# Two experts' rows summed on chip, the first expert's rows by products, and output parts between state-space steps, in a two-block model on one core

## The chip, the cores and the metric

The kernel runs on one core of a Trainium2 chip. A core has a matrix engine (TensorE, PE in the rows, with PEld for its weight loads), three engines for elementwise work (VectorE, DVE; ScalarE, ACT; GpSimd, POOL), one that issues transfers (SyncE, SP), 16 DMA engines, an on-chip memory of 128 partitions and matmul banks of 128 x 512 float32. The metric is the time of one execution of the whole program on the device, in microseconds (us); less is better. All data are float32.

## The reference

Two transformer blocks for 512 tokens of 1024 channels. The first is an RWKV-7 mixer beside banded attention. The second is a mixer of three parts (a state-space mixer with 8 heads in 4 chunks, forgetting attention, a gated convolution) whose 1024 channels go through an output matrix, and then a mixture of 32 experts. What the change touches:

```python
    y = jnp.concatenate([y_ssd, y_att, y_cnv], axis=-1)      # 512 + 256 + 256 channels
    x = x + g_m * (y @ w_out)
    h = rms_norm_2(x, norm_ffn_g) * (1.0 + sc_f) + sh_f
    # router: a group by softmax of h @ w_rg, two of its 8 experts, two weights for each token
    for each expert e (32):                                   # on the rows of h that chose it
        hid = silu(xb @ w_gate[e]) * (xb @ w_up[e])           # 1024 -> 512
        ys  = hid @ w_down[e]                                 # 512 -> 1024
    x = x + g_f * (sum over a token's two experts of weight * ys)
    out = rms_norm_2(x, final_norm_g)
```

## The kernel before, in words

**Order.** Each engine runs its own hand-written list (`pe_block2`, `dve_block2`, `pe_experts` and so on) and waits on semaphores where it needs another's work. Matmul banks are handed out by a plan that is made before the program: `plan(name, by)` gives the next fill a bank and says which engine empties it, `plan_held(name)` keeps a bank for a later fill, `fill`, `begin`, `take` and `empty` carry it out.

**Second block, its end.** `ssd_rows(i)` (L2062, L2064) is the state-space step of a pair of heads, i = 0 to 3; it needs the operands that VectorE makes (`s_gm`). Behind each step VectorE gates the rows with z (`ssd_gated`, L2225 to L2228), ScalarE squares them (L1906), and after two steps TensorE sums the squares (`both(("snorm", g), ...)`, L2036, L2037), from which `yT` tiles 0 to 3 are made (L2323). Tiles 4 to 7 of `yT` (attention and convolution) are ready earlier (`s_m1free`). The output matrix is loaded by SyncE (L573, four loads of 1 MB, semaphore `s_wo`) once `s_m1free` is up. `pe_out` makes the output for four token tiles of 128 rows in halves of 512 columns: `pe_out_part(i, t, half, bank, ks, first, last)` (L763) is the product over the channel tiles `ks`. For the first tile `first_tile` makes channels 4 to 7 of both halves, then the sums of squares, then channels 0, 1 and 2, 3. For each tile VectorE adds the gated result to X (L1679, L1680), ScalarE makes the row norm, VectorE scales the rows into `xn_tiles` (L743), GpSimd stores them to memory (`xn_dram`), and TensorE transposes them (L757) for the router's logits (L2095).

**Router.** VectorE makes from the logits, for each of 8 sets of 128 choices (two choices, four tiles), the expert tile `hot_tile` and the position in it `hot_pos` as one-hot rows (L2472 to L2474). A matrix product of the two (L2125) gives `slots`, the token of each of 64 positions of each expert; a second (L2131) gives `places`, where each result row goes. Experts with more than 64 rows get extra tiles (`extras`, `overflow`): 16 at most.

**Experts.** Three weight slots of 12288 columns hold gate/up (`wgu`, two loads of 2 MB each, L2592) and down weights (`wdn`, one load of 2 MB, L2596) of experts e, e+1, e+2. The first two slots are loaded once the router's inputs in them are dead (`s_slots` 2), the third when the block's end is through (`s_slots` 3); later ones when gate/up or down of the expert three before is done. For an expert GpSimd gathers 64 rows of `xn_dram` (L2657), TensorE turns them (`turn_rows`, L2734), VectorE scales them (`rows_in`, L2897, L2899), TensorE makes gate and up (L2744), ScalarE and VectorE the hidden rows, TensorE turns them (L2751) and makes down (L2760), VectorE gates the result (L2921), and GpSimd scatters it to `y_dram` (L2665). TensorE works on expert e's gate/up before e-1's down.

**The end.** The last expert's result is not scattered: a selection matrix (`last_hot`, turned by L2843) times the weights puts its rows where they belong (`add_last`, L2819). The other results are loaded back (L2638); VectorE adds tiles 0 to 2 to X (L2982), TensorE adds X (`add_x`, L2812) and does tile 3 with diagonals (L2837). ScalarE and VectorE norm the rows (L2960, L2974), which go out (L2642).

## Time and profile before

| | us |
|---|---|
| median of three runs | 1473.2 (1470.58 to 1477.06) |
| the profiled execution | 1470.04 |
| its span, first to last instruction | 1468.0 |
| last output part and router logits, to | 905.7 |
| first gate/up product starts | 936.66 |
| last gate/up product ends | 1438.5 |

The profile is one execution. A row of the timeline has start, duration, engine, line of the kernel, operation, what it writes and reads, its shape and how many instructions are merged; in brackets stands how long the engine was idle before it and what ended that. A float32 matmul is two records.

### The profile page before, as it was taken

To read this page: it belongs to the slowest core of one execution; us is meant where nothing else is said; L and a number is where in the kernel's file an instruction comes from. 1 tells how busy PE (TensorE), PEld (TensorE's weight loads), DVE (VectorE), ACT (ScalarE), POOL (GpSimd) and SP (SyncE) were. 2 spreads that over 40 slices of the span, in tenths; PEclk is the share of its full clock that TensorE was granted. 3 is DMA by queue.
4 is the path that set the end of the run, shared out by engine and by line. 5 is a ranking of instruction groups with operands and counts; after the bars stand their busy time and mean duration, and the time that the engine had idled before them with its cause. 6 is when DMAs were issued, how large, how long until landed. Compare 5 with 4: busy or idle time off the path is not lost.

```text
span 1468.0 us, 21300 instructions
## 1 busy us (share of the span) xinstructions
PE 1328.4 (90%) x7646; PEld 658.7 (45%) x7647; DVE 572.7 (39%) x1078; ACT 345.2 (24%) x745; POOL 158.7 (11%) x273
## 2 busy tenths in 40 slices
PE   5989999999999989998999896699899878998887
PEld 2445656568844444446455444333333322333222
DVE  1366373735123343468566734322212121122124
ACT  2222232321234432211454421011101010111012
POOL 4011111102020000000000001211111111111110
PEclk9999999999999999998999997699989999999999
DMA  9151607051171100121110384169999999999994
GB/s 353 72 202 42 256 2 287 2 201 32 30 243 56 33 15 0 34 86 44 58 58 1 129 372 193 36 273 393 401 420 417 408 402 419 423 393 409 411 389 198
DMA packets 40768, 300.71 MB, mean 205 GB/s; under 512 B 8840, under 2 KB 8992, under 8 KB 23792
## 3 DMA queue, kind: packets, MB, share of 16 engines
q1 hardware_dynamic: 32704, 285.12, 49.4%
q0 software_dynamic: 7984, 14.50, 3.3%
q8 instruction: 53, 0.87, 0.2%
q14 instruction: 27, 0.22, 0.0%
HBM read 296.08 MB, written 13.73 MB: 211 GB/s over the span
## 4 chain that ended last, share of the span: by engine, by line
PE 72%; DMA 17%; DVE 7%; issue 2%; ACT 1%; POOL 0%; SPq 0%; DVEq 0%; ACTq 0%; POOLq 0%
PE bank L832 21%; DMA arena<-in_w_down 12%; PE bank L2744 10%; PE bank L763 8%; PE bank L2760 7%; PE bank L878 4%; DVE arena L2167 3%; DMA arena<-in_w_gu 3%; PE bank L841 2%; PE bank L821 2%; DMA arena<-in_w_ada 2%; PE bank L2734 1%; DMA arena<-in_ada_w 1%; PE bank L1060 1%; PE bank L1076 1%
## 5 line engine op out<-in xcount | busy, mean ns | idle before, releaser
L832 PE MATMUL bank<-hT,arena 128*128 128x512 f32 x768 | 341.7, 600 | 0.0
L2744 PE MATMUL bank<-arena,hT 128*64 128x512 f32 x1024 | 233.9, 606 | 24.2 <-DMA arena<-in_w_gu 22.7
L832 PEld LDWEIGHTS bank<-hT,arena 128*128 128x128 f32 x768 | 144.6, 192 | 177.3 <-issue 174.9
L2744 PEld LDWEIGHTS bank<-arena,hT 128*64 128x64 f32 x1024 | 72.0, 139 | 164.4 <-issue 139.1
L2760 PE MATMUL bank<-arena,yT 128*64 128x512 f32 x512 | 128.7, 649 | 14.5 <-DMA arena<-in_w_down 14.4
L763 PE MATMUL bank<-arena,yT 128*128 128x512 f32 x256 | 114.4, 602 | 2.3 <-DVE yT L1633 2.3
L2904 DVE TENSOR_SCALAR hT<-hT 128x256 f32<-128x256 f32 x32 | 9.4, 294 | 247.1 <-ACT hT L2855 247.1
L763 PEld LDWEIGHTS bank<-arena,yT 128*128 128x128 f32 x256 | 48.2, 193 | 60.5 <-issue 56.2
L2760 PEld LDWEIGHTS bank<-arena,yT 128*64 128x64 f32 x512 | 36.7, 148 | 82.3 <-issue 64.6
L878 PEld LDWEIGHTS bank<-arena 64*64 64x64 f32 x1856 | 59.3, 135 | 27.9 <-issue 14.4
L2855 ACT ACTIVATE hT<-bank 128x256 f32<-128x256 f32 x32 | 12.3, 383 | 246.2 <-PE bank L2744 246.2
L878 PE MATMUL bank<-arena 64*64 64x64 f32 x1856 | 63.9, 220 | 6.5 <-POOLq L673 3.9
L821 PE MATMUL bank<-arena,cactB 128*32 128x512 f32 x288 | 46.0, 665 | 19.5 <-DMA arena<-in_w_ada 17.6
L672 POOL TENSOR_TENSOR arena<-arena 128x512 f32<-128x512 f32 x20 | 29.3, 1467 | 280.6 <-DVEq L1540 194.1
L2921 DVE TENSOR_TENSOR hT<-bank,masks 128x512 f32<-128x512 f32 x32 | 22.1, 692 | 76.7 <-PE bank L2760 76.7
L1808 ACT ACTIVATE arena<-bank 128x512 f32<-128x512 f32 (+4 forms) x53 | 26.0, 491 | 93.4 <-PE bank L832 78.3
L2863 ACT ACTIVATE yT<-bank 128x256 f32<-128x256 f32 x32 | 12.3, 383 | 146.3 <-PE bank L2751 146.3
L2167 DVE SCALAR_TENSOR_TENSOR arena<-arena,cols 128x512 f32<-128x512 f32 x60 | 45.1, 752 | 2.1
L2734 PEld LDWEIGHTS bank<-ident,yT 64*128 64x128 f32 x256 | 30.7, 201 | 33.6 <-issue 33.6
L841 PE MATMUL bank<-arena,hT 128*128 128x128 f32 x384 | 44.0, 276 | 0.0
L841 PEld LDWEIGHTS bank<-arena,hT 128*128 128x128 f32 x384 | 43.4, 192 | 1.3 <-issue 1.1
L2662 POOL CAST place_col<-iotas 128x1 uint32 (+1 forms) x34 | 6.2, 183 | 344.0 <-DVE hT L2921 258.1
(471 smaller groups left out, 1592.1 us busy)
## 6 DMA issues: line engine op xcount, KB each, us to landing
arena<-in_w_gu SPq DMA_DIRECT2D x64, 2048.0 KB, 30.7
arena<-in_w_down SPq DMA_DIRECT2D x32, 2048.0 KB, 36.6
arena<-in_w_in SPq DMA_DIRECT2D x55, 512.0 KB, 3.7
arena<-in_ada_w SPq DMA_DIRECT2D x24, 1024.0 KB, 5.0
arena<-in_w_ada SPq DMA_DIRECT2D x8, 1024.0 KB, 9.1
arena<-in_w_out SPq DMA_DIRECT2D x8, 1024.0 KB, 14.3
arena<-in_w_ada SPq DMA_DIRECT2D x8, 512.0 KB, 4.7
arena<-expert_rows SPq DMA_DIRECT2D x4, 1024.0 KB, 8.4
```

The lines of the kernel that those rows point to most:

```text
L672: done(G.tensor_tensor(Lfc[l % 2], LTc, level_up[:, l:l + 1, 0:HD].to_broadcast([P, 8, HD]), MUL))
L763: ins = T.matmul(bank[:, :], yT[:, k, CH(t)], w_outs[i][:, k, 512 * half:512 * half + 512], start=first and not m, stop=last and m == len( ...
L821: last = T.matmul(banks[ADA_BANK][32 * j:32 * j + 32, :], cactB[:, c0 + k, :], ada_slots[slot][:, j * 512:(j + 1) * 512], start=k == 0, st ...
L832: last = T.matmul(bank[0:rows, :], w[:, k, 0:rows], hT[:, k, :], start=k == 0, stop=k == KD - 1)
L841: last = T.matmul(bank[:, CH(t)], src[:, k, CH(t)], w[:, k, :], start=k == 0, stop=k == KD - 1)
L878: last = T.matmul(bank[r, BK(m)], stat[r, m, :], mov[r, m, :], start=True, stop=True)
L1808: empty(S, "act", S.activation(dst, bank[:, :] if src is None else src(bank), kw.pop("func", ACT.Copy), **kw), name)
L2167: dve.done(V.scalar_tensor_tensor(cv[:, i, :], un[:, i, j:j + SEQ], w(j), cv[:, i, :], MUL, ADD))
L2734: last = T.transpose(banks[bank][:, MT * k:MT * k + MT], tile.xg[:, k::KD], ident[0:MT, 0:MT])
L2744: last = T.matmul(banks[1 + ub][MT * h:MT * h + MT, :], tile.xT[:, k, :], wgu[u][:, k // 4, :, k % 4, 256 * h:256 * h + 256], start=k == 0 ...
L2760: last = T.matmul(banks[5 + (u if db is None else db)][MT * q:MT * q + MT, :], tile.hidT[:, j, h, :], wdn[u][:, a, 512 * q:512 * q + 512], ...
L2921: V.tensor_tensor(tile.yo, banks[5 + u][:, :], gate_rows, MUL).then_inc(steps.rows, 1)
```

## The change

Three things are changed, and what makes room for them.

1. Output parts. In the second block the product over channels 4 to 7 of the first token tile no longer runs after the four state-space steps: half 0 runs before step 2, half 1 before step 3, with the wait for the output matrix in front of half 0. Where they stood, channels 4 to 7 of the second tile's half 0 run. Two banks are held for the two halves from those points and one for the third part.
2. First rows. The first expert's 64 rows are not gathered: a selection matrix `first_hot` (two VectorE steps, `hot_of`) times the four normalised token tiles, which now stay on chip in four buffers, gives them turned (32 products of 64 columns). GpSimd gathers from expert 1 on. The second places matrix goes: the slot matrix now holds the choice as well (tokens numbered to 1024), so its values give the places of one half of the columns, and a repeat of it on the other 64 rows, behind the products, gives the other half. Results are laid out choice by choice in `y_dram`.
3. Two last experts. Expert 30's result is not scattered either; both have their selection matrices turned (now just before the last gate/up product, with the final gain's spreading) and are added by `add_last`. The gate/up weights of expert 31 are requested before the down weights of 30.

For room: `gate2` and `out_tmp` move into slot 1's part of the arena, so slot 1's down weights and slot 2's gate/up weights wait for the block's end and slot 2's down weights for the first rows.

```diff
@@ plan
+            if i >= 2:
+                plan_held(("out", 1, 0, i - 2))
             plan(("ys", i), "dve")
...
+        plan_held(("out", 1, 1, 0))
@@ pe_out
+                    begun = (i, t, half) == (1, 1, 0)
+                    pe_out_part(i, t, half, fill(("out", i, t, half)), range(4 if begun else KD), not begun, True)
@@ pe_block2
+                if i == 2:
+                    eng.wait_ge(s_wo, 128)
+                    eng.wait_ge(s_m1free, 1)
+                if i >= 2:
+                    pe_out_part(1, 0, i - 2, begin(("out", 1, 0, i - 2)), (4, 5, 6, 7), True, False)
                 ssd_rows(i)
@@ first_tile
                 two = [fill(("out", 1, 0, half), 1 + half) for half in range(2)]
-                eng.wait_ge(s_m1free, 1)
-                for half in range(2):
-                    pe_out_part(1, 0, half, two[half], (4, 5, 6, 7), True, False)
+                pe_out_part(1, 1, 0, begin(("out", 1, 1, 0)), (4, 5, 6, 7), True, False)
                 eng.wait_ge(s_ysq, 4)
@@ dve_router
             eng.sem_inc(s_hot, 1)
+            hot_of(0, first_hot)
+            eng.sem_inc(s_hot, 1)
...
+        def hot_of(e, out):
+            dve.done(V.scalar_tensor_tensor(hot_last, hot_pos, 0.0, hot_tile[:, :, e:e + 1].to_broadcast([P, KT, MT]), ALU.is_gt, MUL))
+            dve.done(V.tensor_tensor(out, hot_last[:, 0:TT, :], hot_last[:, TT:KT, :], ADD))
@@ sp_experts
-            for u in range(U):
-                eng.wait_ge(s_slots, 2 if u < 2 else 3)
-                load_gate_up(u, u)
-                load_down(u, u)
+            eng.wait_ge(s_slots, 2)
+            load_gate_up(0, 0)
+            load_down(0, 0)
+            load_gate_up(1, 1)
+            eng.wait_ge(s_slots, 3)
+            load_down(1, 1)
+            load_gate_up(2, 2)
+            eng.wait_ge(tiles[0].xf, 2)
+            load_down(2, 2)
@@ pe_experts
+            eng.wait_ge(s_hot, 2)
+            for k in range(KD):
+                for t in range(TT):
+                    last = T.matmul(banks[ROWS_BANK][:, MT * k:MT * k + MT], xn_tiles[1][t][:, k::KD], first_hot[:, t, :],
+                                    start=t == 0, stop=t == TT - 1)
+            last.then_inc(tiles[0].xf, 1)
+            for by in ("act", "dve"):
+                eng.wait_ge(emptied[by], len(given[by]))
+            for n in range(KT):
+                last = T.matmul(banks[4][MT:P, 0:NE + NOV], hot_pos[:, n, :], hot_tile[:, n, :], start=n == 0, stop=n == KT - 1)
@@ after the last expert
             add_x(3, False)
+            eng.wait_ge(first.rows, NE - 1)
+            add_last(0, 0, start=True)
+            add_last(0, 3)
+            eng.wait_ge(first.hidT, NE)
+            add_last(0, 1, start=True)
             finish(LAST[0], LAST[1], NE - 1)
```

The order of TensorE's instructions around the third state-space step (L2051 are the decay rows ahead of it, L2062 and L2064 the step itself), before against after:

```order
 L2064 MATMUL bank<-arena 64x128
 L2051 MATMUL bank<-cactB,side 128x512 x2
+L762 MATMUL bank<-arena,yT 128x512 x4
 L2062 MATMUL bank<-arena 64x128 x3
 L2064 MATMUL bank<-arena 64x128
```

The output part L762 (before L763) now stands between decay rows and step. On TensorE from the slot matrix to the first gate/up product, before (slot matrix, places matrix, the last expert's selection, the turning of the gathered rows, gate/up):

```order
L2125 MATMUL bank<-hT 64x48 x8
L2131 MATMUL bank<-hT 64x48 x16
L2843 MATMUL bank<-ident,hT 64x128 x8
L2734 MATMUL bank<-ident,yT 128x64 x8
L2744 MATMUL bank<-arena,hT 64x512 x16
```

and after (slot matrix, products, second half of the places, gate/up, turning of the extra tile's rows):

```order
L2127 MATMUL bank<-hT 64x48 x8
L2734 MATMUL bank<-hT,arena 128x64 x32
L2740 MATMUL bank<-hT 64x48 x8
L2759 MATMUL bank<-arena,hT 64x512 x16
L2749 MATMUL bank<-ident,side 128x64 x8
```

32 products have come in, eight transposes, eight products and the selection have gone. At TensorE's end, before (turning of the hidden rows, X, down, X, selections, X, diagonals):

```order
L2751 MATMUL bank<-ident,hT 128x128 x2
L2812 MATMUL bank<-X,ident 128x512 x2
L2760 MATMUL bank<-arena,yT 64x512 x8
L2812 MATMUL bank<-X,ident 128x512 x2
L2819 MATMUL bank<-hT,yT 128x512 x4
L2819 MATMUL bank<-hT 128x512 x4
L2812 MATMUL bank<-X,ident 128x512 x4
L2837 MATMUL bank<-arena 128x512 x4
```

and after:

```order
L2766 MATMUL bank<-ident,hT 128x128 x2
L2833 MATMUL bank<-X,ident 128x512 x2
L2841 MATMUL bank<-hT,arena 128x512 x6
L2775 MATMUL bank<-arena,yT 64x512 x8
L2841 MATMUL bank<-hT,arena 128x512 x2
L2833 MATMUL bank<-X,ident 128x512 x2
L2841 MATMUL bank<-hT,arena 128x512 x2
L2833 MATMUL bank<-X,ident 128x512 x2
L2841 MATMUL bank<-hT,arena 128x512 x4
L2833 MATMUL bank<-X,ident 128x512 x2
L2841 MATMUL bank<-hT,arena 128x512 x2
L2860 MATMUL bank<-arena 128x512 x4
```

Three selections of two products have come in front of the last down product (L2775), and five stand behind it instead of four.

## Rows read from the trace of the kernel before

**Rows 1.** The page's first line.

```profile
span 1468.0 us, 21300 instructions
```

**Rows 2.** Busy by stretch: us, engines' busy us (records), TensorE clock, DMA share, GB/s.

```profile
902.00:905.70 3.70, 3.60 (x16) 3.49 (x16) 0.00 (x0) 0.00 (x0) 3.32 (x3) 0.50 0.79 266
...
936.00:942.00 6.00, 5.34 (x14) 1.65 (x16) 0.60 (x1) 0.00 (x0) 3.91 (x8) 0.50 0.20 72
942.00:948.00 6.00, 6.00 (x34) 2.55 (x31) 0.12 (x1) 0.38 (x1) 0.39 (x2) 0.94 0.08 22
...
976.00:1424.00 448.00, 398.44 (x1818) 143.81 (x1817) 99.62 (x191) 50.78 (x127) 72.15 (x123) 0.95 1.01 408
1424.00:1438.00 14.00, 12.25 (x52) 3.83 (x52) 1.17 (x3) 1.09 (x2) 2.27 (x4) 1.00 0.50 207
```

**Rows 3.** Timeline, state-space steps 2 and 3 to the new tile's transposes.

```profile
822.51 1.15 PE L2062 MATMUL bank<-arena 128*64 128x128 f32 x8 [4.29 <-issue]
...
831.03 0.68 PE L2062 MATMUL bank<-arena 128*64 128x128 f32 x8 [2.87 <-issue]
...
832.74 7.13 PE L763 MATMUL bank<-arena,yT 128*128 128x512 f32 x16
...
841.42 13.90 PE L763 MATMUL bank<-arena,yT 128*128 128x512 f32 x32
855.16 1.05 PE L757 MATMUL bank<-ident,arena 128*128 128x128 f32 x8
...
835.99 0.75 DVE L2227 SCALAR_TENSOR_TENSOR arena<-arena,cols,bank 128x512 f32<-128x512 f32 x1
...
837.55 1.38 ACT L1906 ACTIVATE arena<-arena 128x512 f32<-128x512 f32 x2 [0.90 <-DVEq L2229]
...
851.87 0.75 DVE L743 TENSOR_SCALAR arena<-X,small 128x1024 f32<-128x1024 f32 x1 [1.88 <-ACTq L721]
```

**Rows 4.** The four loads of the second output matrix: min/median/max, first and last start.

```profile
L573 SPq DMA_DIRECT2D arena<-in_w_out x4: 379/470/741, 810.5 to 811.9; - x4
...
DMA to landing us min/median/max: 5.0/11.1/14.1
```

**Rows 5.** Timeline, router to the first gate/up product, and two shapes elsewhere.

```profile
921.25 1.94 PE L2125 MATMUL bank<-hT 128*64 128x48 f32 x16 [6.97 <-DVEq L2476]
924.89 3.26 PE L2131 MATMUL bank<-hT 128*64 128x48 f32 x32 [1.70 <-DVEq L2488]
...
923.23 0.20 DVE L2481 TENSOR_SCALAR side<-bank 64x48 f32<-64x48 f32 x1 [1.72 <-PE bank L2125]
...
929.27 0.69 DVE L2495 SCALAR_TENSOR_TENSOR hT<-hT,side 128x512 f32<-128x512 f32 x1
...
936.66 10.08 PE L2744 MATMUL bank<-arena,hT 128*64 128x512 f32 x32 [1.51 <-DVE hT L2899]
...
902.09 3.60 PE L2095 MATMUL bank<-side,hT 128*128 128x36 f32 x16 [1.69 <-ACT hT L727]
...
146.62 2.00 PE L996 MATMUL bank<-arena 128*128 128x64 f32 x16
```

**Rows 6.** SyncE's issues, the last load's landing, and the timeline's end.

```profile
L2592 SPq DMA_DIRECT2D arena<-in_w_gu x3: 333/353/425, 958.2 to 975.6; - x3
...
1407.66 0.33 SPq L2596 DMA_DIRECT2D arena<-in_w_down  x1
...
DMA to landing us min/median/max: 32.2/32.2/32.2
...
1434.89 3.65 PE L2744 MATMUL bank<-arena,hT 128*64 128x512 f32 x16 [1.39 <-DMA arena<-in_w_gu]
...
1444.91 3.65 PE L2760 MATMUL bank<-arena,yT 128*64 128x512 f32 x16
1448.50 1.98 PE L2812 MATMUL bank<-X,ident 128*128 128x512 f32 x4
...
1452.23 1.88 PE L2819 MATMUL bank<-hT 64*128 64x512 f32 x8
...
1457.58 3.60 PE L2837 MATMUL bank<-arena 128*128 128x512 f32 x8
```

More of the change, by code:

```diff
@@ L775, in pe_out @@
                 for half in range(2):
-                    pe_out_part(i, t, half, fill(("out", i, t, half)), range(KD), True, True)
+                    begun = (i, t, half) == (1, 1, 0)
+                    pe_out_part(i, t, half, fill(("out", i, t, half)), range(4 if begun else KD), not begun, True)
                     if t and not half:
@@ L2125, in pe_block2 @@
                 last = T.matmul(bank[0:MT, 0:NE + NOV], hot_pos[:, n, :], hot_tile[:, n, :], start=n == 0, stop=n == 2 * TT - 1)
-            full(last)
-            eng.wait_ge(s_hot, 2)
-            bank = fill(("places",))
-            for q in range(2):
-                for n in range(2 * TT):
-                    last = T.matmul(bank[MT * q:MT * q + MT, 0:NE + NOV], hot_pos[:, n, :], hot_tile[:, n, :], start=n == 0, stop=n == 2 * TT - 1)
             full(last)
@@ L2493, in dve_router, with place_rows, dve_places @@
+        def place_rows(rows, bank):
+            b = bank[rows, 0:NE + NOV]
+            dve.done(V.tensor_scalar(r_place[rows], b, 0.0, 8192.0, ALU.is_equal, MUL))
+            return V.scalar_tensor_tensor(r_place[rows], b, 2.0, r_place[rows], MUL, ADD)
+        def dve_places(eng):
+            eng.wait_ge(s_spread, 1)
+            dve.done(place_rows(slice(MT, P), banks[4]))
+            dve.done(V.tensor_scalar(places, r_place, half_row, None, ADD))
             eng.sem_inc(s_routed, 1)
-            done(V.tensor_tensor(r_q, hot_tile[:, :, NE - 1], wts.rearrange("p k t -> p (k t)"), MUL))
@@ L2581, in extras @@
                     body(o)
+        ROWS_BANK = 7 if bank_of[fill_at[("slots",)]] == 0 else 0
         def sp_experts(eng):
@@ L2797, in body, with spread @@
                     turn_rows(tiles[u1], first, e + 1, it1)
-                if not begun and not last:
+                if last:
+                    eng.wait_ge(s_copied, 1)
+                    overflow(it, u, e)
+                if not begun:
                     finish(it0, u0, e - 1)
-                if last:
-                    eng.wait_ge(s_copied, 2)
-                overflow(it, u, e)
-            def spread_gain():
+                if not last:
+                    overflow(it, u, e)
+            def spread():
                 eng.wait_ge(s_gateB, 16 + 48)
                 for half in range(2):
-                    spread = T.matmul(banks[4 * half][:, :], ones_row, gain_row[:, 512 * half:512 * half + 512], start=True, stop=True)
-                spread.then_inc(s_spread, 1)
+                    T.matmul(banks[half][:, :], ones_row, gain_row[:, 512 * half:512 * half + 512], start=True, stop=True)
+                eng.wait_ge(s_routed, 3)
+                for j in range(2):
+                    for t in range(TT):
+                        for q in range(2):
+                            ins = T.matmul(banks[3 + 2 * j][MT * q:MT * q + MT, CH(t)], last_hot[j][:, t, :], ident[:, :], start=True, stop=True)
+                ins.then_inc(s_spread, 1)
             def add_x(t, stop):
@@ L2839, in sums @@
                 ins.then_inc(s_x3, 1)
-            eng.wait_ge(s_routed, 3)
-            for t in range(TT):
-                for q in range(2):
-                    turned = T.matmul(banks[6][MT * q:MT * q + MT, CH(t)], last_hot[:, t, :], ident[:, :], start=True, stop=True)
-            turned.then_inc(s_spread, 1)
-            turn_rows(tiles[0], first, 0, 0)
             experts(eng, body)
```

172 lines of the change are left out of this document (76 added, 96 removed).

## The prediction

> **What bounds the kernel now.** I read the page's first lines, then the busy shares by stretch, then the SyncE issues, and only then the instructions at the joints. The span is 1468.0 us [rows 1]. Over the stretch from 976 to 1424 us the DMA engines' share is 1.01 at 408 GB/s with TensorE busy 398 us of 448 [rows 2]: the 32 experts' weights stream, 6.3 MB each, sets the pace there. A stream shortens only if it starts earlier or carries less. It starts when slot 0 comes free: the gate/up loads of expert 3 go out at 958.2 and those of expert 4 at 975.6, when slots 0 and 1 are read [rows 6]. So three joints count: the path of TensorE and VectorE before the router (a later router is a later stream), the path from the slot matrix to the end of the first gate/up product, and what follows the last weights, which were issued at 1407.66 and landed 32.2 us later, at 1439.9, here called T [rows 6]. Anything else that the change moves is under the stream.
>
> **The change, part by part: the moved output parts (term A).** Two groups of eight matmul records move in front of the state-space steps 2 and 3, where TensorE idled 4.29 and 2.87 us [rows 3]; a third group of eight moves from tile 1 into the wait for the second norm. Work of 512 columns takes 0.43 us a record at the full clock (13.90 us for 32) [rows 3], so a group is 3.4 us. But the first group now stands behind the wait for all of `w_out`, and step 2 stands behind the group. The last of those four loads was issued at 811.9 and took 14.1 us: it lands at 826.0 [rows 4], 3.5 us after step 2 began. TensorE, which finished its decay rows at 818.2, would idle 7.8 us and come back at the low clock, as it did after the 4.29 us (eight records of step 2 in 1.15 us, against 0.68 us for step 3's) [rows 3]. Between 3.4 us (all at 2.4 GHz) and 6.9 us (all at 1.2 GHz, twice the time) I take 6.0 us for the group, since the first gate/up product, begun at 936.66, ran about 6 us low before it sped up (granted clock 0.50 to 942, 0.94 behind it) [rows 2, 5]. Then: 826.0 + 6.0 = 832.0; step 2, 1.8 us as step 3 took (831.03 to 832.8), 833.8; first norm's sums 1.7, 835.5; second group 3.4, 838.9; step 3 1.8, 840.7; third group 3.4, 844.1. VectorE and ScalarE need 2.9 us after step 3 for gating and squares (835.99 to 838.93 in the trace) [rows 3], so 843.6: hidden. Second norm's sums 1.7 give 845.8, the sixteen records left of tile 0 6.9 give 852.7, and the last eight of tile 1's first half 856.1. The transposes behind them wait for tile 0's normalised rows, which came 4.3 us after its last product (848.3 to 852.6) [rows 3], so 857.0 plus a semaphore; before they began at 855.16. Term A is +2.0 us, ends -0.4 (group all at the full clock: TensorE alone decides) and +2.9. From there to the router the order is the same and TensorE has no idle time, so it carries over in full. The gate row's load moves past the output weights' wait, the normalised rows have four buffers instead of two: both cost nothing, since the rows' VectorE step waited 1.9 us for ScalarE and not for a store [rows 3].
>
> **The first rows by products (term B).** Before, from the end of the slot matrix (921.25 + 1.94 = 923.2) came: half-row fix-up, places matrix (32 records, 3.26 us), the turned selection, the gather, eight transposes, two VectorE steps, and the first gate/up product at 936.66 [rows 5]: 13.5 us. Now: 32 products of 64 columns against 128x128 weights, 64 records. At the full clock such a shape ran 16 records in 2.00 us, hence 8.0 us; at the low clock the nearest shape, 36 columns against the same weights, ran 16 in 3.60 us, hence 14.4 us [rows 5]. I take 14.4: the granted clock was 0.50, the level of 1.2 GHz, in every stretch read from 902 to 942, also in the 3.7 us in which those records kept TensorE 97% busy (3.60 of 3.70) [rows 2]. Behind the products the second places matrix (16 records at 0.10) and VectorE's two steps run side by side, 1.7 us. The first gate/up product then starts at 923.2 + 14.4 + 1.7 = 939.3, not 936.66, and takes the same 10.08 us, as it again begins low. Term B is +2.6 us. Its ends: rising after 6 us of work, 27 records at 0.225 and 37 at 0.125 are 10.7 us, start 935.6, product 7.0 us, together -4.1; full clock throughout, 8.0 us, -6.9. The high end is a strided read of the weights 10% slower, +4.0. The two added VectorE steps for the first selection (0.69 us, as the step at 929.27 does for the last, and one of half the size) lie in VectorE's 1.72 us wait for the slot matrix [rows 5]; without that cover they'd cost 1.2. The extra expert's gather goes out some 6 us earlier, since GpSimd no longer waits for the places matrix; the two scatters of zero rows and the two last selections (about 3 us of VectorE) end before the first gate/up product does. After it, the next joints (overflow product, down, second gate/up) are unchanged, so A + B shifts the stream.
>
> The Trainium skill, in "TensorE: Matmul & The Clock Gate", section "Part 1: The HAM clock gate", says that what warms the array is a time of sustained matmul work, whatever the number of matmuls. By it 14 us of back-to-back products would not stay low and term B would be -4.1; the low row of 36 columns speaks against it but is short. This is the second case below.
>
> **Weight order at the start.** Slot 1's down and slot 2's gate/up wait for the block's end now: 6.3 MB, 15.4 us at 408 GB/s, from about 904 to 920, and slot 2's down goes out after the products, 5.1 us. All three are there long before their experts. Nothing.
>
> **Two last experts on chip (term C).** Expert 30's scatter and its return through memory go, 0.26 MB or 0.6 us of stream. The gate/up weights of expert 31 now come before the down weights of 30: they land at T-10, and one 2 MB load is 5.1 us. TensorE: gate/up 31 (3.65 us a half) is done by T-5; down 30 runs from T-5.1 to T-1.4; transposes 0.7; X of tile 3 1.9; three selections of expert 30 at 0.94 (1.88 us for two) [rows 6] end at T+4.0; down 31, which could start at T, ends at T+7.6. Before it ended at 1448.5, T+8.6. Then gating 0.8, five selections 4.7, three X products 5.5 and the last diagonal 3.6 give T+22.2 against 1461.2, T+21.3: +0.9, less 0.6 of stream: +0.3 us. Ends: -3.7, if the 4.0 us in front of down 31 find room before T; +5.6, if one more spread (1.8 us) and four more selections (3.8 us) all stand in the path. The result loads no longer stand behind expert 30's scatter but behind that of 29, and find half-idle DMA engines (share 0.50 from 1424 to 1438) [rows 2]; but TensorE's chain from down 31 on has no idle time in it [rows 6], so this gives nothing by itself.
>
> **Sum.** +2.0 + 2.6 + 0.3 = +4.9 us on the profiled execution of 1470.04 us (span 1468.0): 1474.9. The median of the three runs is 3.2 us above that execution, so against it I predict 1473.2 + 4.9 = 1478.1 us. A measurement of this kernel can tell about 0.5%, 7.4 us, from no change; the forecast is inside.
>
> **The rivals.** (1) The clock rises during the products: term B is -4.1 and the time 1473.2 + 2.0 - 4.1 + 0.3 = 1471.4. For it: 14 us of unbroken work; against: the stretch at 902. (2) Slower: the tail. TensorE alone decides the end after T, and the change gives it more to do there. It decides from the point at which its queue is still busy when the last weights land; I have it 4.0 us late already. If nothing of the added work hides, term C is +5.6 and the time 1483.4. For it: the last 12.7 us before were one unbroken row of TensorE work [rows 6]; against: TensorE waited 1.39 us and more at each load just before. (3) The moved parts do fill the gaps, because `w_out` lands earlier than in the trace: up to 6.9 us leave the path and the time is 1473.2 - 6.9 + 2.6 + 0.3 = 1469.2. Against it stand the landing row and the wait in front of the group. (4) The tail's added work all finds room before T: term C is -3.7 and the time 1474.1. Faster by over 0.5% takes (1) and (3) together, 1462.5; (1) and (4) give 1467.4.
>
> **How the numbers follow.** Forecast 0.50, (1) 0.22, (2) 0.14, (3) 0.06, (4) 0.08. The range takes in (1), (3) and the high end of terms A and B (1478.1 + 0.9 + 1.4) and (2): 1468 to 1484 us. Above 1480.6 lie most of (2) and about a fifth of the forecast, together 0.23; under 1465.8 two good surprises at once, 0.07; the rest, 0.70, is within 0.5%.
>
> **What would show it.** Term A: TensorE idle until the output weights land, near 826, step 2 ending near 834 and the first transposes of the new tile near 857. Term B: the products' 64 records take 14 us at granted clock 0.50 and the first gate/up product starts about 4.6 us later than 936.66; about 10 us and a clock of 1 are rival 1. The stream: expert 4's gate/up load goes out near 980 and the last weights land near 1444. Term C: the last diagonal product ends some 22 us after that. I am wrong if the DMA share between these falls below 1, since the shift would then not carry over, or if the last weights land earlier than 1440.

## The result, and the profile after

The changed kernel takes 1475.22 us (median of 20 runs, 1472.58 to 1483.85), the kernel before beside it 1469.76 us (20 runs, 1467.45 to 1477.22). The ratio is 1.0043, with a 95% interval of 1.0028 to 1.0058: slower by 4 to 8.5 us. Its middle lies inside the 0.5% that the prediction calls no change, its upper end a little outside. The forecast was +4.9 us, 1478.1 us in a range of 1468 to 1484. The total held; whether the terms did is the question of all that follows.

The first line and three stretches of the profile after (us, busy us of TensorE, its weight loads, VectorE, ScalarE, GpSimd, then TensorE clock, DMA share, GB/s), which answer to [rows 1, 2]:

```profile
span 1476.9 us, 21405 instructions
...
976.00:1424.00 448.00, 396.13 (x1820) 143.00 (x1818) 96.82 (x186) 49.58 (x124) 74.38 (x125) 0.96 0.99 404
982.30:1430.30 448.00, 395.77 (x1818) 142.89 (x1817) 99.03 (x191) 50.39 (x126) 72.21 (x122) 0.96 1.01 409
1424.00:1438.00 14.00, 13.64 (x78) 6.73 (x76) 3.69 (x8) 3.66 (x8) 1.17 (x2) 0.88 0.77 327
```

The prediction gave a DMA share below 1 as a sign of being wrong, and from 976 to 1424 us it is 0.99. But that stretch begins 6.3 us earlier in this stream than it did in the kernel before, whose fifth expert's load went out at 975.58, against 981.87 here. Moved by those 6.3 us (second row), the share is 1.01 at 409 GB/s, as before. The stream is as full, so a shift at its start can carry to its end. The profiled span is 8.9 us longer, but 5.65 us of that stand ahead of all changed code: state-space step 1 starts at 820.15 where it started at 814.50. The comparison below is therefore made from the start of step 1 (its first row in the timeline), and the other 5.65 us are taken up with the first experiment.

The timeline of TensorE after, from the first moved part to the logits (answers to [rows 3]):

```profile
820.15 0.71 PE L2062 MATMUL bank<-arena 128*64 128x128 f32 x8
...
831.15 5.99 PE L762 MATMUL bank<-arena,yT 128*128 128x512 f32 x8 [7.29 <-DMA arena<-in_w_out]
837.07 0.71 PE L2062 MATMUL bank<-arena 128*64 128x128 f32 x8
...
862.44 1.16 PE L756 MATMUL bank<-ident,arena 128*128 128x128 f32 x8 [0.84 <-DVEq L743]
...
908.68 3.60 PE L2100 MATMUL bank<-side,hT 128*128 128x36 f32 x16 [1.69 <-ACT hT L729]
```

TensorE idles 7.29 us until the output weights land, and the first group takes 5.99 us. Step 2 starts 16.92 us behind step 1 (8.01 before), the first transposes of the new tile 42.29 us behind it (40.66 before), the last logits 88.53 (87.59 before).

From the slot matrix to the extra tile's gate/up (answers to [rows 5]):

```profile
927.83 1.94 PE L2127 MATMUL bank<-hT 128*64 128x48 f32 x16 [6.97 <-DVEq L2473]
929.71 15.54 PE L2734 MATMUL bank<-hT,arena 128*128 128x64 f32 x64
945.18 1.84 PE L2740 MATMUL bank<-hT 128*64 128x48 f32 x15
946.76 1.11 PE L2759 MATMUL bank<-arena,hT 128*64 128x512 f32 x1
...
946.92 7.80 PE L2759 MATMUL bank<-arena,hT 128*64 128x512 f32 x31
...
957.34 7.09 PE L2759 MATMUL bank<-arena,side 128*64 128x512 f32 x32 [0.70 <-DVE side L2918]
```

The 64 records of the products take 15.54 us, so the first gate/up product (two rows, from 946.76) starts 18.9 us behind the slot matrix instead of 15.4. But it takes 8.0 us instead of 10.08, and the extra tile's takes 7.09 instead of 8.78.

And the end (answers to [rows 6]):

```profile
1430.47 1.98 PE L2823 MATMUL bank<-yT 1*128 1x512 f32 x4
1432.38 1.30 PE L2828 MATMUL bank<-ident,yT 128*64 128x128 f32 x16
1433.46 1.93 PE L2828 MATMUL bank<-ident,hT 128*64 128x128 f32 x16
1435.17 7.73 PE L2759 MATMUL bank<-arena,hT 128*64 128x512 f32 x32
1442.72 3.60 PE L2775 MATMUL bank<-arena,yT 128*64 128x512 f32 x16
...
1448.35 2.85 PE L2841 MATMUL bank<-hT,arena 64*128 64x512 f32 x12
1451.12 3.65 PE L2775 MATMUL bank<-arena,yT 128*64 128x512 f32 x16
...
1466.40 3.70 PE L2860 MATMUL bank<-arena 128*128 128x512 f32 x8
```

In this trace neither of the two last down products waits for its weights, which landed at 1441.71 and 1446.63. That is not so in all of them. Here the turning of the selections and the gate/up product behind it met a stretch at the low clock, and in seven of the ten traces with the new end they did not. after_again (the first experiment) is one of the seven:

```profile
1440.77 3.65 PE L2775 MATMUL bank<-arena,yT 128*64 128x512 f32 x16 [0.53 <-DMA arena<-in_w_down]
...
1449.22 3.65 PE L2775 MATMUL bank<-arena,yT 128*64 128x512 f32 x16
1453.67 1.13 PE L2841 MATMUL bank<-hT,arena 64*128 64x512 f32 x4 [0.79 <-DVE hT L2940]
...
1464.50 3.70 PE L2860 MATMUL bank<-arena 128*128 128x512 f32 x8
```

There TensorE still waits 0.53 us for the down weights of expert 30, so nothing ahead of that product costs time.

### The profile page after: what moved, and what is told of

It is laid out like the page before. It is cut to its first block, busy times and chain, and to the rows that moved or that the text cites. A ratio compares the mean times of both kernels' runs of the same rounds, so it can differ in the third digit from the quotient of the medians.

```text
span 1476.9 us, 21405 instructions
## 1 busy us (share of the span) xinstructions
PE 1342.5 (91%) x7718; PEld 675.5 (46%) x7719; DVE 575.4 (39%) x1085; ACT 345.5 (23%) x745; POOL 157.7 (11%) x270
## 4 chain that ended last, share of the span: by engine, by line
PE 69%; DMA 20%; DVE 7%; ACT 2%; issue 2%; POOL 0%; SPq 0%; DVEq 0%; ACTq 0%; POOLq 0%
PE bank L832 20%; DMA arena<-in_w_down 16%; PE bank L2759 8%; PE bank L762 7%; PE bank L2775 6%; PE bank L878 4%; DVE arena L2162 3%; PE bank L841 2%; PE bank L821 2%; DMA arena<-in_w_ada 2%; PE bank L2749 1%; PE bank L2734 1%; DMA arena<-in_ada_w 1%; DMA arena<-in_w_out 1%; PE bank L1060 1%
## 5 line engine op out<-in xcount | busy, mean ns | idle before, releaser
L2775 PE MATMUL bank<-arena,yT 128*64 128x512 f32 x512 | 126.5, 639 | 14.5 <-DMA arena<-in_w_down 14.3
L762 PE MATMUL bank<-arena,yT 128*128 128x512 f32 x256 | 117.3, 612 | 9.6 <-DMA arena<-in_w_out 7.3
L762 PEld LDWEIGHTS bank<-arena,yT 128*128 128x128 f32 x256 | 49.0, 196 | 69.6 <-issue 57.2
L2775 PEld LDWEIGHTS bank<-arena,yT 128*64 128x64 f32 x512 | 36.2, 146 | 81.1 <-issue 63.6
L878 PEld LDWEIGHTS bank<-arena 64*64 64x64 f32 x1856 | 60.1, 136 | 27.8 <-issue 14.4
L1520 DVE TENSOR_TENSOR arena<-bank,arena 128x512 f32<-128x512 f32 x32 | 22.1, 692 | 52.9 <-PE bank L878 52.9
```

The costliest lines, as they stand in the source:

```text
L762: ins = T.matmul(bank[:, :], yT[:, k, CH(t)], w_outs[i][:, k, 512 * half:512 * half + 512], start=first and not m, stop=last and m == len( ...
L878: last = T.matmul(bank[r, BK(m)], stat[r, m, :], mov[r, m, :], start=True, stop=True)
L1520: empty(V, "dve", V.tensor_tensor(dst, b3(bank[:, :], HD), dst, ADD), (n, p, l))
L2775: last = T.matmul(banks[5 + (u if db is None else db)][MT * q:MT * q + MT, :], tile.hidT[:, j, h, :], wdn[u][:, a, 512 * q:512 * q + 512], ...
```

## How the runs are compared

All joints below are taken from each run's own TensorE and SyncE timelines. "A" is from the start of step 1 to the start of the last logits, "B" from the start of the slot matrix to the issue of the fifth expert's first gate/up load, "C" from that issue to the end of the span. From the logits to the slot matrix it is 19.15 to 19.17 us in every run but the three with fillers (20.2 to 20.5).

| kernel | A | B | C | ratio to before, 95% interval |
|---|---|---|---|---|
| before | 87.59 | 54.33 | 492.4 | |
| after | 88.53 | 54.04 | 495.0 | 1.0043 (1.0028 to 1.0058) |
| after_again | 88.53 | 54.01 | 495.8 | 1.0012 (0.9990 to 1.0035) |
| a_off | 89.00 | 53.99 | 492.8 | 1.0025 (1.0004 to 1.0046) |
| a_late | 86.04 | 53.73 | 494.7 | 1.0000 (0.9981 to 1.0020) |
| c_off | 88.73 | 54.11 | 500.0 | 1.0059 (1.0038 to 1.0080) |
| b_gather | 88.52 | 46.52 | 495.3 | 0.9968 (0.9945 to 0.9991) |
| warm | 88.53 | 55.63 | 494.0 | 1.0075 (1.0046 to 1.0104) |
| gather_late | 85.02 | 46.95 | 495.3 | 0.9965 (0.9947 to 0.9983) |
| all_warm | 86.02 | 55.45 | 496.2 | 1.0027 (1.0005 to 1.0048) |
| c_undo | 88.50 | 53.99 | 491.3 | 1.0004 (0.9978 to 1.0031) |
| best | 85.11 | 46.67 | 491.7 | 0.9950 (0.9921 to 0.9978) |
| straight | 88.59 | 53.21 | 494.4 | 1.0009 (0.9981 to 1.0037) |
| straight_warm | 88.81 | 45.38 | 493.6 | 0.9991 (0.9966 to 1.0016) |

In the first pair the sum is +0.94 (A), -0.29 (B) and +2.6 (C), +3.25 us. The times alone can't carry much: an interval of 0.2% to either side is 3 us, and the recorded ratio and the quotient of the two medians differ by up to 0.2% (after_again: 1.0012, and 1474.97 over 1470.06 is 1.0033). What is concluded below rests on joints, and the times are used as a bound.

## Experiment 1: the changed kernel again (after_again)

> The changed kernel once more, beside the kernel before on the same chip, for a second trace. In the first pair of traces the changed kernel was already 5.65 us late at the first state-space step of block 2, ahead of anything that was changed there. Theory R (block 1 just varies from run to run): the time is 4 to 6 us above before, but this offset is another one, inside -3 to +3 us. Theory L (something of the change reaches back into block 1, by the place of data or code): it is again 4 us or more. From that step on both say the same: +0.9 us at the router's logits, +0.6 at the fifth expert's load, +3.3 at the end.

Measured: 1474.97 us, ratio 1.0012; step 1 starts at 817.54, 3.0 us later than in the trace of before, and not 5.65. From there A, B and the sum to the end (657.5 against 656.75) repeat to 0.7 us. Over the thirteen traces that share the changed kernel's block 1, step 1 starts between 813.2 and 825.6 (a_late and best), and a_late, with the same block 1 as the others, is 1.3 us earlier than before. So the offset comes and goes from one execution to the next, as theory R has it. This run alone would not have told, since 3.04 us lies between R's 3 and L's 4. Whether some 2 to 3 us of it are lasting stays open, since the median of the thirteen is 817.1 against one trace of before; the gap between the two medians (5.5 us) is 2.2 us more than the 3.25 us that the changed code shows.

## Experiments 2 and 3: the moved output parts

The first puts the parts back behind the four steps:

```diff
-                if i == 2:
-                    eng.wait_ge(s_wo, 128)
-                    eng.wait_ge(s_m1free, 1)
-                if i >= 2:
-                    pe_out_part(1, 0, i - 2, ...)
...
-                pe_out_part(1, 1, 0, ...)
+                eng.wait_ge(s_m1free, 1)
+                for half in range(2):
+                    pe_out_part(1, 0, half, two[half], (4, 5, 6, 7), True, False)
```

> The changed kernel with the output parts back behind the four state-space steps (part 1 of the change undone). Forecast theory, term A: the parts ahead of steps 2 and 3 cost because the first one waits for the output weights; the logits then come earlier by 0.9 us (what the first pair of traces shows) to 2.0 us (what the sum had), and the time falls by as much. Rival: the cost beside the wait is that the second tile's first half is begun early and finished late; then undoing brings no more than 0.3 us.

Measured: the logits come 0.47 us later, not earlier, and the time is the same (1.0025 against 1.0012, intervals that overlap). Yet its TensorE order is that of the kernel before, whose logits came 1.4 us sooner. The difference arises in step 3 alone. Timeline and stretch of a_off, and the stretch of before (us, TensorE busy, granted clock, DMA share, GB/s):

```profile
833.67 1.15 PE L2058 MATMUL bank<-arena 128*64 128x128 f32 x8 [2.61 <-issue]
...
833.60:836.80 3.20, 3.13 (x29) 0.52 0.00 0
```

```profile
831.00:832.70 1.70, 1.67 (x28) 1.00 0.00 0
```

The same 28 records ran at 1.2 GHz here and at 2.4 GHz there; from step 1 to the start of step 3 both took 16.5 us. So by the trace of before part 1 costs 0.9 us, by a_off's it gains 0.5. Its price is about nothing, and the clock's level in step 3 decides its sign. The expected 0.9 to 2.0 us did not come.

The second keeps the wait for the output weights out of step 2's way:

```diff
-                if i == 2:
+                if i == 3:
                     eng.wait_ge(s_wo, 128)
                     eng.wait_ge(s_m1free, 1)
-                if i >= 2:
-                    pe_out_part(1, 0, i - 2, ...)
+                    pe_out_part(1, 0, 0, ...)
...
+                pe_out_part(1, 0, 1, two[1], (4, 5, 6, 7), True, False)
                 pe_out_part(1, 1, 0, ...)
```

> The changed kernel, but no output part ahead of state-space step 2; half 0 stands ahead of step 3, where the output weights have landed, half 1 and the third part stand in the wait for the second norm. Forecast theory (term A is the wait for the weights): step 2 starts 8.0 us behind step 1, not 16.9, the logits come 2.5 us earlier (1 to 4), and the time falls by that, since one group of 3.4 to 6 us now fills TensorE's 2.87 us of idleness ahead of step 3. Rival (the groups' own time is the cost, the wait is not): logits and time move by less than 0.5 us.

```profile
821.20 1.15 PE L2062 MATMUL bank<-arena 128*64 128x128 f32 x8 [4.28 <-issue]
...
826.95 3.60 PE L762 MATMUL bank<-arena,yT 128*128 128x512 f32 x8
830.47 0.71 PE L2062 MATMUL bank<-arena 128*64 128x128 f32 x8
```

Measured: step 2 is back at 8.0 us behind step 1, and the group ahead of step 3 runs in 3.60 us with no idle time before it; step 3 starts 17.3 us behind step 1, against 24.0 in the changed kernel. The logits come 2.5 us sooner here and in all_warm, 3.4 and 3.5 in best and gather_late, which have the same edit: 85.0 to 86.0 us in the four, 88.5 to 88.8 in the eight with part 1 as changed. The time is 1471.1 against 1475.0 us, ratios 1.0000 and 1.0012, with intervals that overlap. The expectation held in the trace: the wait for the weights is what ate the gain of the other parts. (The edit also moves half 1 into the wait for the second norm, which no run does by itself.)

## Experiment 4: the first rows gathered again (b_gather)

```diff
-            for k in range(KD):
-                for t in range(TT):
-                    last = T.matmul(banks[ROWS_BANK][:, MT * k:MT * k + MT], xn_tiles[1][t][:, k::KD], first_hot[:, t, :], ...)
...
-            gather(tiles[1], 1, 1, s_picked[0], 0)
+            for u in range(2):
+                eng.wait_ge(tiles[u].xf, 1)
+                gather(tiles[u], u, u, s_picked[0], u)
...
+            turn_rows(tiles[0], first, 0, 0, ROWS_BANK)
```

> The changed kernel with the first expert's rows gathered from memory and turned again, the gather issued right behind the slot matrix; no products with the selection. Forecast theory (term B is the products at the low clock): slot matrix to gather's issue 4.3 us, landing 3.2 us later, turning and scaling 2.5 to 3.0 us, so the first gate/up product starts 10.5 us behind the slot matrix's start instead of 18.9, takes 10 us instead of 7.9, and ends 6.3 us earlier; the time falls by 6 us. Rival (the stream is not set by this joint): the first gate/up ends early, but the fifth expert's load goes out at the same time as before and the time moves by less than 1 us.

TensorE of b_gather, then the copy of the gather's list on GpSimd in b_gather and in the kernel before:

```profile
926.93 1.94 PE L2127 MATMUL bank<-hT 128*64 128x48 f32 x16 [6.97 <-DVEq L2473]
...
937.82 8.49 PE L2752 MATMUL bank<-arena,hT 128*64 128x512 f32 x32 [1.51 <-DVE hT L2912]
...
948.91 7.09 PE L2752 MATMUL bank<-arena,side 128*64 128x512 f32 x32 [0.70 <-DVE side L2912]
```

```profile
930.08 0.18 POOL L2662 COPY idx_col<-slots 64x1 uint32<-64x1 uint32 x1 [17.76 <-DVEq L2483]
```

```profile
928.84 0.18 POOL L2654 COPY idx_col<-slots 64x1 uint32<-64x1 uint32 x1 [23.02 <-PEq L2723]
```

Measured: the first gate/up starts 10.9 us behind the slot matrix (18.9 with the products, 15.4 before), and B is 46.5 us, 7.5 under the changed kernel and 7.8 under the kernel before. The time, 1467.3 us at a ratio of 0.9968, is below both. The first gate/up product took 8.5 us and not the expected 10, so it ends 7.5 us earlier than in the changed kernel instead of 6.3. The joint's gain reaches the stream; the rival fell.

The comparison with the kernel before splits part 2 into two halves that had cancelled. The gather of the kernel before was issued so late because of a signal of TensorE's that stood behind the second places matrix and behind VectorE's reading of it: the list was copied 7.6 us behind the slot matrix's start, here 3.2 us. That gives 4.5 us at the start of the first gate/up product, 1.6 in it (8.49 against 10.08 us) and 1.7 in the extra tile's (7.09 against 8.78), together 7.8. The products in place of the gather then cost 7.5. Two things went with the change, though: the matrix, and the place of the signal, which now stands ahead of TensorE's wait for empty banks (`tile.xf` in `pe_experts`). The list itself was written at 923.7 in the kernel before, 5 us before it was copied. No run moves the signal alone, so how much of the 7.8 us needs the matrix gone stays open.

## Experiments 5 and 6: is it the clock? (warm, all_warm)

Fifteen products that nothing reads fill the router's idle times:

```diff
+            for n in range(7):
+                T.matmul(banks[ROWS_BANK][:, :], tri[:, 0, :], X[:, 0, 0:512], start=True, stop=True)
             eng.wait_ge(s_chosen, 1)
...
+            for n in range(8):
+                T.matmul(banks[ROWS_BANK][:, :], tri[:, 0, :], X[:, 0, 0:512], start=True, stop=True)
             eng.wait_ge(s_hot, 1)
```

> The changed kernel with 15 products of 512 columns that nothing reads in TensorE's two idle times of the router (7 ahead of the rank product, 8 ahead of the slot matrix). If the products of the first rows are slow only by the clock (theory of term B), the granted clock is 1.00 when they start, their 64 records take 8.0 us instead of 15.5, the first gate/up 7.0 us instead of 7.9, and the time falls by 8 to 9 us. Rival (this form, weights of 128 x 128 read with a stride against 64 columns, is slow by itself, and the clock does not rise in it): the products take 13 us or more and the time moves by less than 2 us.

The products in warm's timeline, and two stretches of its products alone (us, TensorE and its weight loads, granted clock, DMA share, GB/s):

```profile
927.08 1.13 PE L2132 MATMUL bank<-hT 128*64 128x48 f32 x16
928.38 15.49 PE L2737 MATMUL bank<-hT,arena 128*128 128x64 f32 x64 [0.17 <-DVEq L2480]
```

```profile
928.38:932.50 4.12, 4.12 (x18) 4.12 (x18) 1.00 0.02 4
932.50:943.87 11.37, 11.36 (x48) 11.18 (x47) 0.51 0.14 40
```

The fillers did their work: the slot matrix ran in 1.13 us instead of 1.94, and the products began at 2.4 GHz. They still took 15.49 us. A record started every 0.238 us at a granted clock of 1.00 and every 0.239 at 0.50; and after some 4.3 us of products without a gap the clock fell (4.1 in all_warm). So the clock, on which the price and the first rival both rested, has nothing to do with the length of these products. The first gate/up met the low clock and took 9.3 us instead of 8.0, and B is 1.6 us longer. Ahead of B the fillers held the slot matrix up by 1.3 us. The ratio is 1.0075, from six runs; that is more than these 2.9 us over the changed kernel, and the rest stays open.

> The products that nothing reads in the router's idle times, and no output part ahead of state-space step 2. If both theories hold, 8.5 + 2.5 = 11 us under the changed kernel, 5.5 us under the kernel before (0.996 of it), the lowest of these kernels.

Measured: 1475.7 us, ratio 1.0027; A 2.5 us shorter, B 1.4 us longer. The part of the expectation that a_late carries came; the 8.5 us from the clock did not.

## Experiments 7 and 8: is it the stride? (straight, straight_warm)

```diff
-                    last = T.matmul(banks[ROWS_BANK][:, MT * k:MT * k + MT], xn_tiles[1][t][:, k::KD], first_hot[:, t, :],
+                    last = T.matmul(banks[ROWS_BANK][:, MT * k:MT * k + MT], xn_tiles[1][t][:, P * k:P * k + P], first_hot[:, t, :],
```

> The changed kernel, but the products of the first rows read their weights as 128 columns that lie side by side, not every eighth (it gives the first expert other channels in the wrong order, so its rows are not the reference's). The products took 0.242 us a record at granted clock 0.50, and also in the 3.4 us at clock 1.00 that the filled router gave them. Theory S (the stride in the weights' read sets this, not the clock): a record takes 0.12 to 0.13 us where the clock is 1.00 and 0.20 to 0.23 where it is 0.50; started at 0.50, the 64 take 13 to 14.5 us, and the time falls by 1 to 2.5 us. Rival F (128 x 128 weights against 64 columns cost this whatever the stride): 15.5 us and the same time.

> The same unstrided read, with the 15 products that nothing reads in the router's idle times. Theory S: the products start at clock 1.00 and take 8.0 us if it stays there, 10 to 12 us if it falls under way as it did in the strided run, and the time falls by 3.5 to 8 us against the run with the fillers alone. Rival F: 15.5 us, and the time stays.

The products in straight with their stretch, and the products and first gate/up in straight_warm with the stretch of the products:

```profile
926.71 13.92 PE L2734 MATMUL bank<-hT,arena 128*128 128x64 f32 x64
...
926.70:940.50 13.80, 13.80 (x65) 0.50 0.12 34
```

```profile
925.77 7.36 PE L2737 MATMUL bank<-hT,arena 128*128 128x64 f32 x64 [0.17 <-DVEq L2480]
...
934.63 7.09 PE L2762 MATMUL bank<-arena,hT 128*64 128x512 f32 x32 [0.45 <-DVE hT L2921]
...
925.80:933.10 7.30, 7.30 (x65) 1.00 0.10 25
```

Theory S holds and the form rival is out, by the products' own rows. A record starts every 0.213 us at 0.50 and every 0.112 at 1.00: unstrided, the products follow the clock. The clock itself keeps the level at which they began: it stays up through them in straight_warm, and stays at 0.50 through 13.8 us of them in straight. Read every eighth column, they take 0.238 at either level, 12% more at 1.2 GHz and 2.1 times as much at 2.4 GHz. B is 53.2 us in straight (0.8 less than after) and 45.4 in straight_warm (10.3 less than warm). In straight the first gate/up starts 1.6 us sooner behind the slot matrix but takes 0.8 longer, since the clock rose 3.3 us into it and not 1.7. The times go the same way. Straight is at 1.0009 against 1.0012 for after_again, 0.4 us where 1 to 2.5 were expected. With fillers it is 1.0075 with the stride and 0.9991 without, more than the expected 3.5 to 8 us.

## Experiments 9 and 10: the end (c_off, c_undo)

In c_off expert 30's result is scattered again, its three selections ahead of the last down product and one behind it go, and all orders stay as changed:

```diff
-                if not (isinstance(e, int) and e in (0, NE - 1)):
+                if not (isinstance(e, int) and e == 0):
                     it0, u0 = before(it, u)
                     scatter(tiles[u0], first, u0, e - 1, s_placed_col[0], e - 1)
...
-            add_last(0, 0, start=True)
-            add_last(0, 3)
-            add_last(0, 1, start=True)
```

> The changed kernel, with expert 30's result scattered and loaded back again; only the last expert's stays on chip, and the order of the last weights stays as changed. Forecast theory, term C: three selections ahead of the last down product, one selection's turning (1.3 us) and one selection behind it leave TensorE's last row of work; the last diagonal product starts 2 to 4 us earlier behind the last weights' landing, against 0.6 us more of stream: the time falls by 1.5 to 3 us. Rival (the results' loads bound the end: they stand behind the scatter of expert 30 again): the last addition of VectorE, not TensorE, ends later and the time does not fall, or rises by up to 3 us.

TensorE and VectorE of c_off behind the last weights:

```profile
1444.95 3.65 PE L2775 MATMUL bank<-arena,yT 128*64 128x512 f32 x16
1455.78 2.08 PE L2841 MATMUL bank<-hT,arena 64*128 64x512 f32 x4 [7.17 <-DVE hT L2934]
```

```profile
1452.20 2.60 DVE L2997 SCALAR_TENSOR_TENSOR X<-arena,wts,X 128x1024 f32<-128x1024 f32 x2 [8.37 <-DMA arena<-expert_rows]
1455.03 0.69 DVE L2934 TENSOR_TENSOR hT<-bank,masks 128x512 f32<-128x512 f32 x1 [0.22 <-DVE X L2997]
```

Measured: 1480.3 us, 1.0059; C is 500.0 us, 5 more. The rival holds, with more than its 3 us and with a link that it had not named: the result loads now wait for a scatter that is issued at 1444.95, VectorE's list has the first addition ahead of the gating of the last result, and that gating ends at 1455.7, 7.1 us behind the down product. So, given the changed order of weights and this order in VectorE's list, keeping expert 30 on chip does spare about 5 us. That says nothing yet on part 3 as a whole, since the order is a part of it; c_undo takes that back too:

```diff
+                if last_but_one:
+                    next_down()
                 if not (isinstance(e, int) and e == NE - 1):
                     next_gate_up(after(it, u)[1], e + 1)
...
                 if last:
+                    finish(it0, u0, e - 1)
                     spread()
```

> The changed kernel with part 3 undone whole: expert 30's result scattered, its down weights ahead of expert 31's gate/up, its down product ahead of the last gate/up, and the sums in the order of the kernel before; only the last selection is still turned in front of the last gate/up product and not in the router. Forecast theory (term C measured in the first pair as +2.2 us behind the last weights and -0.6 of stream; what the earlier run without expert 30 on chip lost was VectorE's gating of the last result behind a late load): the last diagonal product starts 17.5 to 18.5 us behind the last weights' landing instead of 19.8, and the time falls by 1 to 2 us. Rival (keeping expert 30 on chip pays by itself): the time rises by 1 us or more.

```profile
1426.06 3.65 PE L2785 MATMUL bank<-arena,yT 128*64 128x512 f32 x16 [0.67 <-DMA arena<-in_w_down]
...
1436.61 3.65 PE L2769 MATMUL bank<-arena,hT 128*64 128x512 f32 x16 [0.53 <-DMA arena<-in_w_gu]
...
1443.23 1.88 PE L2842 MATMUL bank<-X,ident 128*128 128x512 f32 x4
1445.05 3.65 PE L2785 MATMUL bank<-arena,yT 128*64 128x512 f32 x16
...
1457.72 3.60 PE L2867 MATMUL bank<-arena 128*128 128x512 f32 x8
```

Measured: 1472.3 us, 1.0004; C is 491.3 us, 3.7 under the first trace of the changed kernel. C is 491.3 to 492.4 us in the three kernels with the old end (before, c_undo, best) and 492.8 to 496.2 in the ten with the new one: means of 491.8 and 494.7. Part 3 costs 2.9 us.

The last diagonal product starts 16.1 us behind the last weights' landing (1441.58), earlier than the 17.5 to 18.5 expected, and 16.2 in best. The kernel before took 17.7, but its trace had a low clock in one place where these two had the high one (0.56 from 1441.72 to 1444.90):

```profile
1441.72 3.26 PE L2812 MATMUL bank<-X,ident 128*128 128x512 f32 x4
```

With the new end the figure is 18.8 to 18.9 us in the seven traces like after_again and 19.7 to 19.8 in the three with a low stretch. So at the high clock the new end is 2.7 us longer than the old, and all of it stands behind the last down product. That product starts 3.5 us behind the landing in c_undo (1445.05) and in after_again (1449.22, landing 1445.68) alike. From its start to the last diagonal product it is 12.7 us in c_undo and 15.3 in after_again: 0.8 us of waiting for the gating of the last result, which the old order filled with a product of X, 1.5 us for the fifth selection and for taking them in smaller groups, and 0.3 us in the products of X.

## Experiments 11 and 12: the parts together (gather_late, best)

> Both edits together: the first rows gathered, and no output part ahead of state-space step 2. If the two joints add, the time is 6 + 2.5 = 8.5 us under the changed kernel and 3 us under the kernel before (0.998 of it). If the gain of one is given back at the other, it is within 1 us of the run with the gather alone.

Measured: 1466.1 us, ratio 0.9965. Both joints keep their own gain (A 3.5 us, B 7.1 us shorter than after). The time is 1.2 us under b_gather's and the ratios are 0.9965 and 0.9968, so by the times alone the expectation's two cases are not told apart.

> The first rows gathered, no output part ahead of state-space step 2, and part 3 undone whole. If the three add up, 1 to 2 us under the run with the first two (0.9965 of before), so 0.9955. If the end is bound otherwise, within 0.5 us of that run or above it.

The last diagonal product of best:

```profile
1457.87 3.60 PE L2860 MATMUL bank<-arena 128*128 128x512 f32 x8
```

Measured: 1466.08 us, ratio 0.9950 (0.9921 to 0.9978), the lowest of all, faster than both kernels. From step 1 to the end it takes 642.6 us, against 653.5 before and 656.75 after. Its profiled run had lost over 8 us in block 1, which is why this row stands as late as in c_undo. Whether it also beats gather_late in time these intervals can't tell; by the joints it does, by 3.9 us.

## Why the prediction was right, and where it was not

**What bounds the kernel: right.** Three joints and a full stream between them. B changed by -7.5 us in b_gather and C did not move (495.3 against 495.0), so a shift at the start carries to the end. Expert 4's load went out at 981.9 (near 980 by the prediction) and the last weights landed at 1446.6 (1444).

**Term A, +2.0: mechanism right, size too large.** TensorE did idle until the output weights landed, the group took 5.99 us (6.0 taken), step 2 started 16.9 us behind step 1 and the transposes 42.3 (42.5 by the sum's 857.0). The step that failed is "it carries over in full": the last tile's transposes, 1.97 us at the low clock before, took 1.16 at the high one, and 0.94 us were left at the logits. a_off then showed that even this is no more than the clock's level in step 3 of the kernel before. What stands is the cost against the better place: 2.5 to 3.5 us.

**Term B, +2.6: right in its rows, wrong in its reason, and wrong in its sum.** 14.4 us were taken, 15.5 measured. The price was read from a low-clock row of 36 columns, and the trace agreed with it because the clock was low: at that level unstrided products of this very form take 13.9 us (straight), and the stride adds 12%. What sets their length at either level, the stride, was in the text only as a possible 10% on top. By the Trainium skill, "TensorE: Matmul & The Clock Gate", section "Part 1: The HAM clock gate", a long enough time of sustained matmul work lifts the clock. Here 15.5 us of products without a gap stayed at 0.50 where they began there, and the clock fell where they began at 1.00. The unstrided ones began at 0.50 in straight and stayed there too, for 13.8 us. The traces do not agree with the page for products of this form, strided or not. The step that failed in the sum is "takes the same 10.08 us, as it again begins low": the clock rose 1.7 us into it, and the extra tile's product behind it no longer met a low stretch. These gave 2.1 and 1.7 us back: -0.3 us at the stream, not +2.6. And the working never asked what the rest of the edit, without the places matrix on the path, was worth with the gather kept; that was 7.8 us.

**Term C, +0.3: wrong in size, +2.9 measured.** The chain of the new end was nearly right: the last diagonal product was to start 18.6 us behind the landing (T+22.2 less its 3.6), and seven traces have 18.8 or 18.9. The step that failed is the comparison with "T+21.3" before. That trace had lost 1.6 us to a low clock, 1.4 of them in its product of X, so the 1.0 us that the sum gained ahead of the last down product (T+7.6 against T+8.6) isn't there: at the high clock that product starts at T+3.5 in both orders. Another low stretch, ahead of the last gate/up product, gave the first trace of the changed kernel its 19.8. Behind the down product, 1.9 us were taken (11.0 against the 9.1 of before) and 2.6 measured. And the 0.6 us of saved stream can't be seen: from the fifth expert's load to the last landing it is 463.5 to 466.9 us in the fourteen traces, with no order by part 3.

**Rivals.** (1) is out with its mechanism: no clock would have sped these products. (2), the longer tail, is what happened, at half its price: the work that the change put ahead of the last down product did hide in seven of ten traces (1 us of it showed in the other three), the work behind it did not. (3) and (4) did not come.

**Together** the sum of terms was +4.9 and the changed code shows +3.25 in the first pair (+0.9, -0.3, +2.6), with some 2 us of the gap between the medians ahead of it and open. The forecast's total was good by luck: A and B were too dear, by 1.1 and 2.9 us, and C too cheap by 2.3.

## What to carry to other kernels

Price a removed operation by itself, with everything else kept: here one half of an edit was worth 7.8 us and the other cost 7.5, and the whole looked like nothing. Before a term is taken as the difference of two ends, look whether both ends ran at the same granted clock: one stretch of 3.4 us at the low level in the trace of before was worth more than the term. And put work in front of a step only when all that it waits for has landed by then: one step later the same eight records held step 3 up by 0.7 us (17.3 us behind step 1, 16.5 before) and took 3.6 us of work from behind it.

## What the runs showed of the hardware

- Weights of 128 x 128 float32 read every eighth column: one record in 0.238 us at a granted clock of 1.00 and of 0.50 alike; read side by side, 0.112 and 0.213 us.
- Begun at a granted clock of 1.00, the strided products saw it fall to 0.50 after 4.3 us (warm) and 4.1 us (all_warm) without a gap on TensorE; in the unstrided ones it stayed at 1.00 for all of their 7.3 us. Begun at 0.50, neither saw it rise, in 15.5 us (after) and 13.8 us (straight).
- The same instructions in the same order reached the logits 87.6 and 89.0 us behind step 1, by the clock's level in one 3 us stretch. An effect of 1 us at such a joint isn't shown by one pair of traces.
